# Two decoder blocks on one core: the RWKV-7 recurrence begins behind the value block, with the streams of XBC and Z between its steps

## The reference

```python
h = rms_norm(x, norm_mix_g); u = h @ w_in      # columns: z | xbc | dt | r k v | pw pa pg
# SSD
xbc = silu(causal_depthwise_conv(xbc, conv_w, conv_b))         # 4 taps and a bias
xdt = xs * dt; cs = cumsum(dt * a)
y_diag = einsum(cm @ bm, exp(cs_l - cs_s) masked, xdt)
y = (y_diag + y_off + xs * d_skip) * silu(z)    # then a norm by group, gain norm_g
# RWKV-7
uf = uf + (u_prev - uf) * mu                    # token mix of r, k, v, pw, pa, pg
kk = k * k_k; kk = kk / max(sqrt(sum(kk * kk, by head)), 1e-12)
k = k * (1 + (iclr - 1) * k_a)
state = state * w_t + (state @ -kk_t) * (kk_t * a_t) + v_t * k_t;  y_t = state @ r_t
bonus = sum(r * k * r_k, by head) * v
x = x + concat(y_ssd, y_rwkv) @ w_out
```

## Time and profile before

| | |
|---|---|
| median of 3 runs | 2846.21 us |
| span of the profiled execution | 2846.5 us |
| TensorE busy | 2803.9 us (99%) |
| VectorE busy | 1735.5 us (61%) |
| ScalarE busy | 1315.8 us (46%) |
| granted TensorE clock, mean | 0.997 |
| streams of XBC and Z | 186 to 302.5 us |
| recurrence beside SSD | 302.5 to 448.3 us |

### The profile page before, as it was taken

The page is one execution under the profiler, slowest core; times in us unless marked ns, Lnnn a source line. Parts: engine busy times, 40 slices in busy tenths (PEclk is TensorE's granted clock), DMA queues, the critical chain, the costliest instruction groups (busy, mean ns, idle before and its releaser), DMA issues.

```text
span 2846.5 us, 40996 instructions
## 1 busy us (share of the span) xinstructions
PE 2803.9 (99%) x17275; PEld 2398.9 (84%) x17275; DVE 1735.5 (61%) x2053; ACT 1315.8 (46%) x1672; POOL 43.6 (2%) x71
## 2 busy tenths in 40 slices
PE   8999899999999999999999999999999999999998
PEld 7888788788888888888888888888888888888886
DVE  5688666654445555555555666655666756665665
ACT  6445333544434443444434545644554444443444
POOL 2000000000000000000000100000000000000001
PEclk9999999999999999999999999999999999999999
DMA  7565214555545656655666555555456555555553
GB/s 232 177 193 176 77 47 150 186 182 192 179 135 183 186 192 192 191 193 183 197 190 189 189 180 190 178 169 174 161 180 198 185 195 190 187 198 192 190 181 132
DMA packets 392420, 504.60 MB, mean 177 GB/s; under 512 B 11360, under 2 KB 285293, under 8 KB 391213
## 3 DMA queue, kind: packets, MB, share of 16 engines
q1 hardware_dynamic: 385149, 490.35, 53.5%
q10 hardware_dynamic: 7088, 11.62, 1.3%
HBM read 499.77 MB, written 2.17 MB: 176 GB/s over the span
## 4 chain that ended last, share of the span: by engine, by line
PE 95%; DVE 3%; ACT 1%; issue 1%; DMA 0%; ACTq 0%; SPq 0%; DVEq 0%
PE PS L639 37%; PE PS L644 33%; PE PS L648 17%; PE PS L864 3%; PE PS L676 1%; DVE wlo L1889 1%; PE PS L996 0%; PE PS L1012 0%; PE PS L804 0%; PE PS L784 0%; PE PS L1045 0%; DMA slab<-in_x 0%; ACT whi L1287 0%; PE PS L819 0%; PE PS L1036 0%
## 5 line engine op out<-in xcount | busy, mean ns | idle before, releaser
L1889 DVE TENSOR_TENSOR wlo<-raw,whi 128x1024 fp32r<-128x1024 f32 x922 | 1127.0, 1228 | 791.1 <-ACT whi L1287 787.5
L1287 ACT ACTIVATE whi<-raw 128x1024 fp32r<-128x1024 f32 x922 | 970.3, 1057 | 963.3 <-PE PS L648 497.9
L644 PE MATMUL PS<-XX,whi 128*128 128x512 f32 (+1 forms) x3856 | 1216.8, 397 | 0.0
L648 PEld LDWEIGHTS PS<-XX,wlo 128*128 128x128 f32 (+1 forms) x3856 | 724.5, 188 | 171.3
L648 PE MATMUL PS<-XX,wlo 128*128 128x256 f32 (+1 forms) x3856 | 759.7, 278 | 0.0
L639 PE MATMUL PS<-whi,act 128*128 128x512 f32 x2240 | 602.1, 391 | 0.0
L644 PEld LDWEIGHTS PS<-XX,whi 128*128 128x128 f32 (+1 forms) x3856 | 589.3, 189 | 2.8 <-DVE wlo L1889 0.6
L639 PEld LDWEIGHTS PS<-whi,act 128*128 128x128 f32 x2240 | 418.0, 188 | 85.3
L639 PE MATMUL PS<-wlo,act 128*128 128x512 f32 x1120 | 344.9, 389 | 0.0
L639 PE MATMUL PS<-whi,XX 128*128 128x512 f32 x1024 | 280.8, 396 | 6.5 <-DVE wlo L1889 5.1
L639 PEld LDWEIGHTS PS<-wlo,act 128*128 128x128 f32 x1120 | 210.2, 188 | 44.0
(11 more groups left out here) (363 smaller groups left out, 1355.5 us busy)
## 6 DMA issues: line engine op xcount, KB each, us to landing
raw<-in_ffn_w SPq DMA_DIRECT2D x128, 1024.0 KB, 5.5
raw<-in_w_in SPq DMA_DIRECT2D x103, 1024.0 KB, 5.0
raw<-in_w_ffn_gate SPq DMA_DIRECT2D x44, 1024.0 KB, 4.9
raw<-in_w_ffn_up SPq DMA_DIRECT2D x44, 1024.0 KB, 4.9
raw<-in_w_ffn_down SPq DMA_DIRECT2D x44, 1024.0 KB, 5.1
raw<-in_w_out SPq DMA_DIRECT2D x32, 1024.0 KB, 5.1
raw<-in_xattn_wk SPq DMA_DIRECT2D x16, 1024.0 KB, 5.2
raw<-in_xattn_wv SPq DMA_DIRECT2D x16, 1024.0 KB, 5.0
```

The lines of the kernel that those rows point to most:

```text
L644: T.matmul(ps[0:wd, f, :], whi[:, o:o + wd], b.x[:, kk, :], start=first, stop=False, skip_group_check=True)
L648: mm = T.matmul(ps[0:wd, f, 0:SEQ], wlo[:, o:o + wd], b.x[:, kk, 0:SEQ], start=False, stop=last, skip_group_check=True)
L1287: S.activation(k.whi[:, h % 4, 0:b.size], k.raw[:, t % 4, u * b.size:(u + 1) * b.size], ACT.Copy).then_inc(k.w_hi, 1)
L1889: V.tensor_tensor(k.wlo[:, h % 4, 0:b.size], k.raw[:, h // 2 % 4, u * b.size:(u + 1) * b.size], k.whi[:, h % 4, 0:b.size].bitcast(F32), AL ...
```

## The change

In words:
- **Order of blocks.** The six rkv blocks take their columns by the table (2, 3, 0, 1, 4, 5): k first, then r, then v. lora is spread up to rkv1+6, prep to rkv3+6 and the end of rkv5.
- **Work moved to ScalarE.** The token mix is now 4 scaled copies on ScalarE (L1379) and one pass of 4 on VectorE (L2012). Conv tap 0 and bias are 4 activations (L1388). KK = K * k_k (L1648, 8 copies) and the key gain 1 + (iclr - 1) k_a (L1628, 8) are ScalarE's. r_k is folded into the selection matrix of the bonus sum. The three exponentials (L1619, L1621, L1624) go from prep to the end of lora.
- **The recurrence** starts behind rkv5 (half 56). Its steps make `ROUNDS` = 44 rounds; up to `filled(n)` halves of the stream stand behind step n, in pieces of half a half (`parts`), 40 in all: 24 of XBC by round 14, 8 of Z up to round 26, 8 more up to round 37, none in rounds 37 to 43.
- **SSD** steps stand in rounds by the tables SSD_PE, SSD_ACT and SSD_DVE. Its products use PSUM banks 2 and 3 alone, and both Z blocks banks 0 and 1. The transposes of y (L825) go two banks by turns, between the last round and the first halves of w_out (`joined`). The decays' DMAs are issued by ScalarE (`decays_laid`).
- `chunk_own` is new SBUF for what the recurrence kept in buffers of x. The DMA scratch is 1024 bytes.

The number of matrix products of each kind stays the same.

```diff
-LORA_STEPS, PREP_STEPS = 13, 18
+LORA_STEPS, PREP_STEPS, KEY_STEPS = 17, 13, 9
-SSD_STEPS = 33
+ROUNDS = 44
+SSD_PE = (18, 19, 20, 20, 23, 25, 27, 29, 31, 34, 36, 38, 40)
+SSD_ACT = (18, 19, 20, 23, 23, 25, 27, 29, 31, 34, 36, 38, 42, 43)
...
-        for j in range(6):
-            put("rkv", j, w, 2576 + 512 * j, "feat", rows=True)
+        for j, cols in enumerate((2, 3, 0, 1, 4, 5)):
+            put("rkv", j, w, 2576 + 512 * cols, "feat", rows=True, cols=cols)
...
+def filled(n):
+    if n < 15:
+        return 2 + 22 * n / 14
+    return 24 + (8 * (n - 14) / 11 if n < 26 else 8) + (0.8 * (n - 26) if n > 26 else 0) if n < 37 else 40
+def joined(s, post_steps, ssd_steps):
+    next(post_steps)
+    for m in range(4):
+        next(ssd_steps)
+        next(ssd_steps, None)
+        if m:
+            s.go(1)
+    run(ssd_steps)
...
     T.wait_ge(*k.rp.DVE("end"))
     T.wait_ge(*k.ri.DVE("z"))
-    steps = side_by_side(ssd_steps, chunk_steps)
-    advance(steps, SSD_STEPS - 1)
-    T.wait_ge(*k.sd.DVE("xl7"))
-    run(steps)
+    for n in range(ROUNDS):
+        next(chunk_steps)
+        s.parts_to(2 * first + int(2 * filled(n)))
+        advance(ssd_steps, SSD_PE.count(n))
+    run(chunk_steps)
+    joined(s, halves_of(post_pe, k), ssd_steps)
...
     yield from step_sizes_act(k)
+    S.wait_ge(*rp.DVE("lwd"))
+    S.activation(k.LW, k.LW, ACT.Exp, scale=-DECAY).then_inc(rp.act, 1)
+    yield
+    S.activation(k.end_decay, k.cum, ACT.Exp, scale=-DECAY).then_inc(rp.act, 1)
+    S.wait_ge(*rp.ACT("e2"))
+    yield
+    S.activation(k.cum, k.cum, ACT.Exp, scale=DECAY).then_inc(rp.act, 1)
+    yield
+    S.wait_ge(k.rest_made, 1)
+    for f in range(RP):
+        ins = S.activation(k.key_gain[:, f, :], k.IC[:, f, :], ACT.Identity, scale=k.col["rwkv_k_a"][:, f:f + 1],
+                           bias=k.rest[:, f:f + 1])
...
 def prep_act(k):
     S, rp = k.nc.scalar, k.rp
-    S.wait_ge(*rp.DVE("kr"))
+    S.wait_ge(*k.mix.DVE("m", 1))
+    for f in range(RP):
+        ins = S.activation(k.KK[:, f, :], k.RKV[:, 8 + f, :], ACT.Copy, scale=k.col["rwkv_k_k"][:, f:f + 1])
+    ins.then_inc(rp.act, 1)
+    S.wait_ge(*rp.ACT("kr"))
     S.activation(k.t1, k.KK, ACT.Square).then_inc(rp.act, 1)
...
+            for f in range(4):
+                at = 4 * j + f
+                ins = S.activation(o[:, f, :], k.buf3[:, f, 0:SEQ], ACT.Identity, scale=k.col["ssd_conv_w"][:, at:at + 1],
+                                   bias=k.col["ssd_conv_b"][:, at:at + 1])
...
+    prepared(s, lora_dve(k), prep_dve(k))
     V.wait_ge(*k.rp.DVE("end"))
     V.memset(k.St, 0.0).then_inc(k.ri.dve, 1)
+    s.flush()
...
-            if t == behind_chunks:
-                decays_sync(k)
```

More of the change, by code:

```diff
@@ L424, in put @@
                     more["acted"] = next(func) if "func" in arg else None
-                b = Block(kind, j, w, k0, kt, col, mode, x, there, part, len(self.blocks), self.tiles, more)
+                number = len(self.blocks)
+                parity = self.blocks[-1].parity if kind == "tok" and "alone" in more else number % 2
+                b = Block(kind, j, w, k0, kt, col, mode, x, there, part, number, self.tiles, parity,
+                          len([o for o in self.blocks if o.parity == parity]), more)
                 col += b.ncol
@@ L442, in plan @@
         for j in range(2):
-            put("tok", j, w, 512 * j, "tok", dst=self.Z, func=ACT.Silu, row=0)
+            put("tok", j, w, 512 * j, "tok", dst=self.Z, func=ACT.Silu, row=0, **({"alone": True} if j else {}))
         w = i["w_out"][0]
@@ L620, with parts_to, parts @@
 class TensorStream(Stream):
+    part = None
     def half(self, h):
+        run(self.parts(h))
+    def parts_to(self, n):
+        while 2 * self.at + (self.part is not None) < n:
+            if self.part is None:
+                self.part = self.parts(self.at)
+                next(self.part)
+            else:
+                run(self.part)
+                self.part, self.made, self.at = None, self.at + 1, self.at + 1
+    def parts(self, h):
         k = self.k
@@ L624, in half @@
         ps = k.PS[:, 2 * b.parity:2 * b.parity + 2, :]
-        if h == b.first and b.number >= 2:
+        if h == b.first and b.turn:
             T.wait_ge(*k.free(b))
@@ L825, in lora_pe @@
     yield from step_sizes_pe(k)
+    for _ in range(5):
+        yield
 def prep_pe(k):
@@ L833, in prep_pe @@
     head_sum(k, k.t1, 4).then_inc(rp.pe, 1)
-    for _ in range(6):
+    for _ in range(9):
         yield
     T.wait_ge(*rp.DVE("rk"))
-    head_sum(k, k.t1, 4).then_inc(rp.pe, 1)
-    for _ in range(11):
-        yield
+    T.wait_ge(k.rest_made, 2)
+    head_sum(k, k.t1, 4, sel=k.sel_rk).then_inc(rp.pe, 1)
+    yield
+    yield
+    yield
 def chunk_pe(k, c, grp):
@@ L1519, in ssd_act @@
     yield
-    yield
     S.wait_ge(*sd.DVE("rs"))
     S.activation(rs[:, :, 0:2], rs[:, :, 0:2], ACT.Sqrt).then_inc(sd.act, 1)
-    for _ in range(4):
-        yield
+    yield
     gain = k.col["ssd_norm_g"]
@@ L1574, in prep_act @@
     norms_laid(k, 0, k.norm_rows, slice(0, SEQ))
-    for _ in range(6):
+    for _ in range(8):
         yield
```

393 lines of the change are left out of this document (191 added, 202 removed).

## The result

| | before | changed |
|---|---|---|
| median | 2845.55 us (4 runs, 2843.56 to 2848.19) | 2869.89 us (4 runs, 2867.37 to 2870.79) |
| ratio | | 1.0086, 95% interval 1.0074 to 1.0098 |
| profiled span | 2846.5 us | 2868.8 us |
| TensorE busy, idle | 2803.9, 42.6 us | 2816.3, 52.5 us |

What follows compares the result with a forecast made beforehand. TensorE was taken to bound the kernel (95% of the chain). Old idle -16.6, new idle +17.2, changes between product kinds +4.9 and clock 0 gave +5.5 on 2846.5, so 2852 us, range 2838 to 2863.

Steps and rivals of the forecast that it cites:

- step 1: Norm's head sum in the rkv stream: TensorE waits for ScalarE's square behind its queue, 6.6 us together (5.0 to 7.6).
- step 7: Clock: the half-clock stretch at 347 us goes (-3.4), one behind the head sum's wait comes (+3.4), net 0.
- The first product: Start of the recurrence: its first products wait for the state's memset behind VectorE's last rkv evacuation, 2.8 us (2.5 to 3.3).
- XBC's ends: Ends of XBC blocks: the chunk's evacuations come late behind the conv taps in two of three blocks, 3.2 us (0 to 6).
- The rounds with little stream: Rounds 38 to 43 have no stream, so waits of about a microsecond stay there, 1.7 us (0.5 to 4).
- The joint: Recurrence's end into w_out: last state's wait 1.1 us, transposes of y on two banks 1.8; together 2.9 us.
- The SSD products: In the recurrence: they now run a round behind VectorE, so their 4.6 us of waits (L784) go.
- Step 6: Recurrence: 19 more changes between 64x64 and 128x128 products, about 0.26 us each, cost 4.9 us (3 to 8).
- A: The forecast's own sum of waits, changes between product kinds and clock: 2852 us, range 2847 to 2858; chance 0.45.
- B: ScalarE is in time: head sum waits at most 2.3 us, no half-clock stretch follows; 2838 us, chance 0.27.
- C: Waits are as counted, but the clock stays, so its 3.4 us are not lost; 2848.5 us, chance 0.13.
- D: VectorE is late in the filled rounds, half a microsecond in each of 37; 2870 us, chance 0.15.

Runs made afterwards that it cites:

- fillers: The changed kernel with 22, 26 and 56 transposes that nobody reads ahead of TensorE's three waits in lora and prep; 2862.57 us (1.0061).
- xbc_first: all_later with the 24 halves of XBC ahead of the recurrence's first step and rounds 0 to 14 bare; 2856.48 us (1.0038).
- tuned: all_later with memset_early's edit, VectorE's tap 0 wait and ScalarE's SiLU a step later, key gain in two pieces, ScalarE's sums a step later; 2843.59 us.
- norm_later: The changed kernel with the norm's head sum and all that hangs on it two steps later; 2868.09 us (1.0078).
- all_later: The changed kernel with the edits of lora_later and norm_later, and the three exponentials spread over earlier steps of lora; 2857.83 us (1.0046).
- filler: The changed kernel with 56 transposes that nobody reads ahead of TensorE's wait for the norm's square only; 2867.76 us (1.0078).
- lora_later: The changed kernel with lora one step later on three engines and TensorE's cumulative sum a step behind VectorE's; 2861.03 us (1.0055).
- memset_early: The changed kernel with the state's memset moved to the end of prep, ahead of the last block's wlo and evacuation; 2863.34 us (1.0060).
- before_mem: The kernel before with only the norm of the memory moved three halves later in the w_out stream; 2844.23 us (0.9998).

## Why the prediction was wrong

The steps that failed are the scope of step 1, which took the rest of the rkv stream as free of waits (two more came, 6.1 us), and step 7, which let the clock come out at nothing (it cost 8.6 us).

- **The places of the recurrence's waits: right.** The first product waits 2.9 (2.8 forecast). XBC's ends cost 2.6 + 1.2 = 3.8 us (3.2). The rounds with little stream cost 3.1 (1.7), with two waits of 0.7 and 0.6 that the list above leaves out. The joint costs 2.0 (2.9). Together that is 11.8 against 10.6. The SSD products don't wait.
- **Step 1, the head sum: right in mechanism, a little short.** It waits 7.2 us (6.1), with 0.8 at a wlo on the way (0.5): 8.0 us, above the 5.0 to 7.6 of its range. ScalarE's queue in the changed kernel:

```profile
104.27 0.60 ACT L1366 ACTIVATE slab<-PS 128x512 f32<-128x512 f32 x1 [1.68 <-PE PS L680]
107.07 0.37 ACT L1534 ACTIVATE slab<-PS 16x256 f32<-16x256 f32 x1 [2.20 <-DVE slab L2215]
...
107.82 1.28 ACT L1537 ACT_TABLE_LOAD   x1 [0.38 <-ACT slab L1534]
...
110.32 1.69 ACT L1379 ACTIVATE slab<-slab,one_less 128x256 f32<-128x256 f32 x4
111.92 1.91 ACT L1619 ACTIVATE slab<-slab 128x2048 f32<-128x2048 f32 x1
...
117.56 1.91 ACT L1624 ACTIVATE chunk_own<-chunk_own 128x2048 f32<-128x2048 f32 x1
...
120.79 4.04 ACT L1628 ACTIVATE slab<-slab,one_less,param_cols 128x256 f32<-128x256 f32 x8
...
126.62 3.29 ACT L1648 ACTIVATE slab<-slab,param_cols 128x256 f32<-128x256 f32 x8
129.95 1.91 ACT L1651 ACTIVATE slab<-slab 128x2048 f32<-128x2048 f32 x1
```

 From the evacuation to the end of the square it is 27.6 us, where I had 26.1. The term that was too small is the copy: 1.69 for four, 4.04 for eight with a bias, 3.29 for eight without, so 0.41 to 0.51 each, beyond my upper bound of 0.39, and 9.0 for the twenty where I had 6.8. I had bounded it by an activation from PSUM and by a quarter of a longer one. The Trainium skill has the size: "ScalarE: Activation LUTs", section "What ACT_TABLE_LOAD costs", gives 186 ns and 0.833 ns an element, 93 ns more for each per-partition operand, and an overlap of 93. An estimate from these figures is 0.40 us with a scale and 0.49 with a scale and a bias, and the trace agrees (0.41 and 0.51). Of the drain of 1.4 us in the same section the trace shows nothing here either: 1.28 for the load and 0.38 ahead of it.
- **The same step, its scope: wrong, and the first cause.** I counted the one wait that stood behind the most work and took the rest of the compressed stretch as free. "LORA_STEPS 17" up to half 30 instead of 13 steps up to half 40 also brought two products to the place where their input had not arrived. In the kernel before, ScalarE's sigmoid (L1536, now L1605) was done just ahead of the products that need it (L819, now L849):

```profile
49.26 0.63 ACT L1536 ACTIVATE slab<-slab 128x512 f32<-128x512 f32 x1
...
49.95 3.72 PE L819 MATMUL PS<-slab 96*128 96x256 f32 x16
```

 In the changed kernel TensorE is there one half earlier, at 47.18 us, and the sigmoid is not (it ends at 50.05). VectorE's ten small steps ahead of L763 run from 92.21 to 94.55 us, behind the wlo that precedes them, and TensorE is there at 91.39. Both could have been read from the order of instructions with rows of the trace before. These 6.1 us are most of the missing idle time.
- **Step 7, the clock: wrong, and the larger cause.** I gave back one stretch and took one, net 0; it is +8.6. I had tied each stretch to a gap and allowed one, although my own sum had gaps of 6, 2.8 and 2 us. The one that I gave back did go (3.2 us by its busy time); the one at the head sum cost 1.3, since most of it lay in the wait. What came besides are 5.9 us behind the two waits that I had not counted, 1.4 at the recurrence's first product and 3.0 among its last products. fillers shows the cause for the rkv stream: with TensorE busy in the three waits 14.5 us of busy time went back to full clock, and the median fell by 7.3 us.
- **Step 6, the changes between kinds of product: right**, 3.8 us for 19 more (4.9). That is 0.20 each, and 0.21 by xbc_first, against 0.26. That the tiling mode drains TensorE, as the Trainium skill has it ("TensorEngine Tiling (Array Packing)", section "Key Properties"), agrees with it in sign. By itself it is no reason to avoid mixing: tuned hides 10.2 us of idle time in the recurrence's stage for these 3.8.
- **The rivals.** A's mechanism held for the waits that it counted, and its sum was 17 us short, 6 by waits that I had not counted, 3 by others' sizes, 9 by the clock, less 1 on the changes. B fell with the head sum's wait; it also took no gap to be longer than 2.37 us while its own sum held 2.8 at the recurrence's start. C fell with the stretches at half clock. D, VectorE late in every filled round, didn't occur: three waits of 4.4 us in 37 rounds. That its 2870 is the measured time is chance. The range failed because all cases shared the assumption that the rkv stream held one wait.

## What to carry to other kernels

When work is compressed to let something start earlier, list every product in the compressed stretch and ask for each whether its input is there, not only for the one with the most ahead of it: here three waits of 13 us in all and their 7 us of clock made most of the 24 us, and without them the change is level. A wait behind a full queue of another engine moved when its reader was moved (norm_later); spreading the work of that queue ended it (tuned). And price a long wait of TensorE at its length and, by these traces, up to 3 us more for the clock behind it; a few products that nobody reads, in the wait, are a quick test of that share.

## What was not expected

- Whether a gap of 1.5 to 2.6 us brings a stretch at half clock varies between executions and builds. In the traces of all fourteen kernels, from 20 us on, such a stretch began in or at most 1.5 us behind each of the 25 gaps of 2.8 us or more, and with 13 of 16 gaps of 1.9 to 2.6. Behind the 2.6 us of the XBC end near 320 to 330 there was none in the changed kernel and all_later, and one of 3.4 in filler, fillers, lora_later, norm_later and memset_early. In before_mem the same gap as in the earlier trace rows left the clock at 1.00:

```profile
347.46 1.10 PE L784 MATMUL PS<-slab,over_x 128*128 128x64 f32 x8 [2.37 <-DVE over_x L2181]
```

 Behind 1.6 us among the last 64x64 products (ends at 454.1) the changed kernel had 6.8 us at 0.50; tuned had none behind 1.6 and 1.5. So such stretches are worth counting over several kernels before one is charged to a gap. What decides between them stays open.
- With its waits repaired the overlap hides 10 us of idle time and still ends level. The stage ahead keeps 4.0 us more idle time, the changes cost 3.8, and the stage behind, with the joint, has 1.1 more idle. The 3.2 us of half clock that tuned lacks in the recurrence's stage are no firm gain, since before_mem lacks them too. Whether a better placement could keep the rkv stream free of waits, as before, was not tried.
